# Two-layer decoder trunk: weight differences taken two per gate/up pair behind each product, and the first FFN boundary re-ordered

## The reference, cut to what matters

```
x = x + rms_norm(f(rms_norm(x, g_pre)), g_post)

def swiglu(h, w_in, w_out):
    gu = h @ w_in
    g, u = jnp.split(gu, [FFN_HIDDEN], axis=-1)
    return (jax.nn.silu(g) * u) @ w_out
```

## Time and profile before

| what | value |
|---|---|
| median of 3 runs | 1205.3 us (1205.02 to 1206.21) |
| the profiled execution's own time | 1205.84 us |
| its span, first to last instruction | 1203.9 us |
| TensorE busy | 1171.3 us (97%) |
| VectorE, ScalarE, GpSimd busy | 634.5, 445.6, 485.9 us |
| mean granted TensorE clock | 0.992 |

### The profile page before, as it was taken

One profiled execution on the slowest core, in us unless ns is written; L12 is line 12 of the kernel. 1 busy time (PEld: TensorE's weight loads), 2 busy tenths in 40 slices (PEclk: granted clock), 3 DMA queues, 4 the chain that ended last, 5 costly groups with the idle time before them and its releaser, 6 DMA issues.

```text
span 1203.9 us, 13773 instructions
## 1 busy us (share of the span) xinstructions
PE 1171.3 (97%) x5434; PEld 966.6 (80%) x5434; DVE 634.5 (53%) x783; ACT 445.6 (37%) x681; POOL 485.9 (40%) x268
## 2 busy tenths in 40 slices
PE   8999999998999999999979999999989999999998
PEld 6888887896887888888768888778968788888886
DVE  3441056274344655677365844734635356556773
ACT  5122336442222222365434333644322232225642
POOL 5546521745355544200647443023545454441004
PEclk9999999998999999999989999999999999999999
DMA  7444203256776233466644233112576752325663
GB/s 269 130 126 143 99 3 103 71 193 254 289 294 235 96 105 88 114 193 193 220 162 149 97 131 115 35 53 73 213 309 245 278 210 87 105 87 149 192 194 120
DMA packets 53085, 187.30 MB, mean 156 GB/s; under 512 B 4739, under 2 KB 4995, under 8 KB 52780
## 3 DMA queue, kind: packets, MB, share of 16 engines
q1 hardware_dynamic: 48760, 173.38, 42.4%
q10 hardware_dynamic: 4276, 13.26, 3.7%
HBM read 160.13 MB, written 26.49 MB: 155 GB/s over the span
## 4 chain that ended last, share of the span: by engine, by line
PE 78%; DMA 12%; DVE 8%; POOL 1%; ACT 1%; issue 0%; SPq 0%; DVEq 0%; POOLq 0%
PE ps L1255 23%; PE ps L1257 23%; PE ps L1256 23%; DMA stage<-fold_w 6%; DMA fold_t<-stage 5%; DVE stage L950 3%; PE ps L1520 2%; PE ps L1486 2%; DVE stage L948 1%; DVE stage L947 1%; DVE stage L949 1%; PE ps L1504 1%; PE ps L1292 1%; DMA gain_pre<-norms 1%; POOL w_lo L362 0%
## 5 line engine op out<-in xcount | busy, mean ns | idle before, releaser
L362 POOL TENSOR_TENSOR w_lo<-w_raw,w_hi 128x1024 fp32r<-128x1024 f32 (+1 forms) x179 | 443.2, 2483 | 621.1 <-ACT w_hi L478 619.2
L1255 PE MATMUL ps<-h_hi,w_hi 128*128 128x512 f32 (+1 forms) x1008 | 386.1, 383 | 11.8 <-DVE prod L972 11.8
L478 ACT ACTIVATE w_hi<-w_raw 128x1024 fp32r<-128x1024 f32 x240 | 244.7, 1031 | 388.3 <-DMA w_raw<-weights 313.5
L1256 PE MATMUL ps<-h_lo,w_hi 128*128 128x512 f32 (+1 forms) x1008 | 383.5, 380 | 0.0
L1257 PE MATMUL ps<-h_hi,w_lo 128*128 128x512 f32 (+1 forms) x1008 | 383.4, 380 | 0.0
L1255 PEld LDWEIGHTS ps<-h_hi,w_hi 128*128 128x128 f32 x1008 | 190.5, 189 | 51.2 <-issue 16.1
L1257 PEld LDWEIGHTS ps<-h_hi,w_lo 128*128 128x128 f32 x1008 | 190.5, 189 | 36.3
L1256 PEld LDWEIGHTS ps<-h_lo,w_hi 128*128 128x128 f32 x1008 | 190.6, 189 | 35.7 <-issue 0.2
L972 DVE TENSOR_TENSOR prod<-work,ps 128x512 f32<-128x512 f32 x44 | 30.1, 684 | 195.4 <-ACT work L629 195.4
L1257 PE MATMUL ps<-w_hi,prod_r 128*128 128x512 f32 x308 | 119.9, 389 | 0.0
L1255 PE MATMUL ps<-w_hi,h_hi 128*128 128x512 f32 x288 | 115.2, 400 | 0.4 <-DVE h_lo L867 0.4
(11 more groups left out here) (152 smaller groups left out, 1198.4 us busy)
## 6 DMA issues: line engine op xcount, KB each, us to landing
w_raw<-weights SPq DMA_DIRECT2D x156, 512.0 KB, 4.4
stage<-fold_w SPq DMA_DIRECT2D x10, 2048.0 KB, 8.3
fold_t<-stage SPq DMA_DIRECT2D x10, 2048.0 KB, 7.5
w_raw<-fold_t SPq DMA_DIRECT2D x40, 512.0 KB, 4.2
w_raw<-fold_w SPq DMA_DIRECT2D x30, 512.0 KB, 3.8
x<-x_in SPq DMA_DIRECT2D x4, 512.0 KB, 6.3
gain_post<-norms ACTq DMA_DIRECT2D x4, 512.0 KB, 4.2
stage<-fold_w SPq DMA_DIRECT2D x2, 1024.0 KB, 5.3
```

What stands on the lines that cost most here:

```text
L362: nc.gpsimd.tensor_tensor(w_lo[:, c % RING, 0:n], w_raw[:, c % RING, 0:n], w_hi[:, c % RING, 0:n].bitcast(F32), ALU.subtract).then_inc(lo_ ...
L478: nc.scalar.activation(w_hi[:, c % RING, 0:n], w_raw[:, c % RING, 0:n], ACT.Copy).then_inc(hi_done, 1)
L1255: mm(to, held[0], moved[0], start=start, stop=False, skip_group_check=more)
L1256: mm(to, held[0], moved[1], start=False, stop=False, skip_group_check=more)
```

## The change

Three places are touched.

- **SyncE**: the load of fold j comes behind chunk 8+4j's load instead of chunk 6+4j's, and the store of fold j behind chunk 12+4j's instead of 8+4j's, directly ahead of the load of fold j+1.
- **VectorE**: of each fold, two subtractions come behind product 2j and two behind product 2j+1; the last fold comes whole behind product 10. Each subtraction now also waits for the one before it.
- **Boundary 2**: ScalarE's post squares of tiles 0 and 1 come ahead of `high(V1)`, and the later steps of the chain follow in another order; GpSimd has the two post roots ahead of `low(V1)`; VectorE has the residual of tile 1 ahead of the normed row of tile 0; TensorE has its turn of tile 0 behind column 0 of product 6's last three chunks, and the turn of tile 1 ahead of the last chunk.

```diff
@@ SyncE
-                    j, late = divmod(c - FINS[layer] - 6, 4)
-                    if 0 <= j < FOLDS and late in (0, 2):
+                    j, late = divmod(c - FINS[layer] - 8, 4)
+                    for j, store in ((j - 1, True), (j, False)):
+                        if late or not 0 <= j < FOLDS:
+                            continue
                         part = slice(j * CHUNK, min((j + 1) * CHUNK, FH * SEQ))
                         held = stage[:, :, 0:part.stop - part.start]
-                        if late == 0:
+                        if not store:
 
                             if FOLDS * layer + j:
                                 sp.wait_ge(fold_stored, 16 * (FOLDS * layer + j))
...
@@ GpSimd, boundary
                 half_eps(b)
+                if b == 2:
+                    post_rstds(b, 0)
+                    post_rstds(b, 1)
+                    low(V1)
+                    pre_rstds(b, 0)
+                    pre_rstds(b, 1)
+                    low(V1 + 1)
+                    for t in (2, 3):
+                        post_rstds(b, t)
+                        low(V1 + t)
+                        pre_rstds(b, t)
+                    return
...
-            lows(FOUT0 + 36, V1 + 2)
+            lows(FOUT0 + 36, V1)
...
@@ ScalarE, boundary
+                if b == 2:
+                    sums(0, True, False)
+                    sums(1, True, False)
+                    high(V1)
+                    sums(0, False, True)
+                    sums(1, False, True)
+                    high(V1 + 1)
+                    turned_high(b, 0)
+                    sums(2, True, False)
+                    high(V1 + 2)
+                    turned_high(b, 1)
+                    sums(2, False, True)
+                    sums(3, True, False)
+                    high(V1 + 3)
+                    sums(3, False, True)
+                    turned_high(b, 2)
+                    turned_high(b, 3)
...
             ffn_out(0)
-            highs(V1, V1 + 2)
...
@@ VectorE, boundary
-                for t in range(2):
-                    post(b, t)
-                    pre(b, t)
+                post(b, 0)
+                if b == 2:
+                    post(b, 1)
+                pre(b, 0)
+                if b != 2:
+                    post(b, 1)
+                pre(b, 1)
                 turned_low(b, 0)
...
@@ VectorE, fold and ffn
-            def fold(layer, j):
+            def fold(layer, j, parts):
 
                 n = min(CHUNK, FH * SEQ - j * CHUNK)
                 w11, w12, w21, w22 = (stage[:, i, 0:n] for i in range(4))
-                vec.wait_ge(fold_landed, 16 * (FOLDS * layer + j + 1))
-                own(nc.vector.tensor_tensor(w11, w12, w11, ALU.subtract))
-                nc.vector.tensor_tensor(w12, w22, w12, ALU.subtract)
-                own(nc.vector.tensor_tensor(w22, w22, w11, ALU.subtract))
-                nc.vector.tensor_tensor(w21, w21, w22, ALU.subtract).then_inc(folded, 1)
+                if 0 in parts:
+                    vec.wait_ge(fold_landed, 16 * (FOLDS * layer + j + 1))
+                    own(nc.vector.tensor_tensor(w11, w12, w11, ALU.subtract))
+                    own(nc.vector.tensor_tensor(w12, w22, w12, ALU.subtract))
+                if 1 in parts:
+                    own(nc.vector.tensor_tensor(w22, w22, w11, ALU.subtract))
+                    nc.vector.tensor_tensor(w21, w21, w22, ALU.subtract).then_inc(folded, 1)
...
                 for p in range(FT):
-                    if p % 2 == 0 and p // 2 < FOLDS:
-                        fold(layer, p // 2)
...
                         nc.vector.tensor_tensor(prod_r[:, LO11, p, :], prod[:, A11, p, :],
                                                 prod_r[:, HI11, p, :].bitcast(F32), ALU.subtract).then_inc(product_ready, 1)
+                        fold(layer, p // 2, (0, 1) if p == FH - 1 else (p % 2,))
...
@@ TensorE, ffn_out
-                for t in range(2):
-                    if b < 4:
-                        turn(b, t)
-                    for i in range(3, 6):
-                        last = chunk(6, i, (4, 6), True, side(5), (t,))
-                        if t == 1:
-                            last.then_inc(chunk_used, 1)
-                    if t == 0:
-                        last.then_inc(y_done, 1)
+                for i in range(3, 6):
+                    last = chunk(6, i, (4, 6), True, side(5), (0,))
+                last.then_inc(y_done, 1)
+                if b < 4:
+                    turn(b, 0)
+                for i in range(3, 6):
+                    if b < 4 and i == 5:
+                        turn(b, 1)
+                    chunk(6, i, (4, 6), True, side(5), (1,)).then_inc(chunk_used, 1)
```

More of the change, by code:

```diff
@@ L416, in boundary @@
                 half_eps(b)
+                if b == 2:
[10 more added lines that the diff above has]
+                    return
                 post_rstds(b, 0)
-                if b in (1, 3):
+                if b < 4:
                     low(AFTER[b] + AHEAD - 1)
@@ L421, in boundary @@
                 for t in range(1, TILES):
-                    if b == 2 and t <= 2:
-                        low(AFTER[b] + t + 1)
                     post_rstds(b, t)
@@ L514, in sum_post_squares @@
                     act.wait_ge(merged, 10 * (b // 2 - 1) + 8 + t + 1)
-                if b == 4:
+                if b == 4 or (b, t) == (2, 1):
                     act.wait_ge(post_summed, q)
@@ L532, in sum_pre_squares @@
                 if b:
-                    act.wait_ge(post_summed, q - 3)
-                elif t:
+                    act.wait_ge(post_summed, q - 2 if (b, t) == (2, 0) else q - 3)
+                if (b, t) == (2, 1) or (t and not b):
                     act.wait_ge(pre_summed, q)
@@ L551, in sums @@
                         sum_pre_squares(b, t)
+                if b == 2:
[15 more added lines that the diff above has]
+                    turned_high(b, 3)
+                    act.wait_ge(x_updated, 4 * b)
+                    act.dma_start(gain_post[:], norms[b, 1].partition_broadcast(P)).then_inc(gain_post_landed, 16)
+                    return
                 sums(0, True, True)
-                if b == 2:
-                    high(AFTER[b] + 2)
                 sums(1, True, True)
-                if b == 2:
-                    high(AFTER[b] + 3)
                 if b == 0:
```

## The result

The changed kernel takes 1210.66 us (median of six runs, 1209.73 to 1211.94) against 1205.16 before: a ratio of 1.0047, 95% interval 1.0034 to 1.0060. It is slower, as forecast, but by 5.5 us and not by 28. Its profiled execution took 1211.13 us with a span of 1209.2. The two parts go opposite ways, as the prediction's sum has them: the boundary gains, the folds lose.

A forecast was written before the change was run, and what follows sets the result against it. The prediction took the one-buffer turn of load, fold, store and next load to bound TensorE: 1205.84 + 38.8 (folds, two FFNs) - 11.0 (boundary 2) = 1233.6, so 1233 us, range 1206 to 1244.

The forecast's parts named there:

- Boundary 2: Where TensorE waits for the normed row `gate_x`: the earlier chain and later turns win the full 11.0 us.
- the second half of the fold: VectorE's last two subtractions of a fold: both stand behind one of GpSimd's and take 6.74 us together.
- two meetings: Forecast's own case: both second-half subtractions wait for GpSimd; about 1224 to 1243 us, chance 0.62.
- one meeting: Rival: VectorE gets in first once, second half 4.5 us, chunk 25 at 404.9; 1211 us, chance 0.18.
- the store of 7.49 us: The fold's store back from the buffer, taken at 7.49 us as one term of each turn.
- the circle: Load, fold, store, next load through one buffer: 27.15 us a turn against 21.76 us for four chunks of TensorE.
- the first wait and its half clock: Layer 0's wait of 4.59 us for the product, and 2.2 us of clock behind it: both gone.
- the last store: End of each FFN's folds: behind chunk 32's load, product 11 waits for it; chunk 25 starts 26.2 us late.
- the loss of 9.0 us per FFN before: What each FFN's waits for the product cost TensorE in the unchanged kernel, read at silu(11): 9.0 us.
- the cover of the turns: `gate_x` of tiles 0 and 1 ready ahead of TensorE's turns, by 1.2 us or more and 1.6 us.

The follow-up runs named there:

- e6: The changed kernel with a short VectorE memset of 128 columns ahead of each split fold's second half, so that GpSimd gets in front: 1232.28 us.
- e4: The changed kernel with each fold whole, all four subtractions behind product 2j, the queue of loads and stores as changed: 1213.91 us.
- e9: The changed kernel with GpSimd's subtraction for chunk 4j+10 held until fold j is done: 1196.93 us.
- e7: The changed boundary, with the folds in eleven parts of 512 columns through both halves of the same buffer: 1175.90 us.
- e3: The changed kernel with the store of fold 5 behind chunk 30's load instead of chunk 32's: 1202.82 us.

## Why the prediction was right and where it went wrong

**The step that failed** is the second half of the fold: "GpSimd is ahead by 0.09 us, and both subtractions of the second half should stand behind one of GpSimd's: 6.74 us". It measured 4.54, with VectorE ahead by 0.08 us. The mechanism was right: whoever is first makes the other wait, and e6 with GpSimd in front gave 1232 us. The lead was read too finely from rows 7, in two ways. First, I took start plus duration of `prod_r` for the time at which VectorE can start, 310.72. In the changed kernel `prod_r` ends by its row at 304.01 + 0.99 = 305.00, and the next instruction, which waits for nothing, starts at 304.93: 0.07 us earlier. Second, the product starts 302.84 - 301.19 = 1.65 us behind the rounding of its chunk, in the earlier trace rows 1.57. GpSimd's next subtraction hangs on a rounding that follows the product, and moves with it; `prod_r`, which takes 0.42 us alone and 0.99 here, ends when GpSimd's earlier subtraction lets it (302.33 + 2.38 = 304.71), and doesn't move. Together 0.15 us, which turn +0.09 into -0.06, near the measured -0.08. This account of the lead is read from the two traces and wasn't tried apart; that the lead decides over 21 us was.

The weight of the two cases was misread, too. The prediction took two meetings "since the same pair of streams met in every turn of the first fold". The second fold of the kernel before looks different, by the timeline of VectorE and GpSimd:

```profile
292.21 1.22 DVE L949 TENSOR_TENSOR stage<-stage 128x1024 f32<-128x1024 f32 x1
293.47 3.30 DVE L950 TENSOR_TENSOR stage<-stage 128x1024 f32<-128x1024 f32 x1
...
292.23 3.45 POOL L362 TENSOR_TENSOR w_lo<-w_raw,w_hi 128x1024 fp32r<-128x1024 f32 x1 [2.86 <-ACT w_hi L478]
```

VectorE is in front by 0.02 us, and only one subtraction meets GpSimd. In the kernel before, the eight full-size folds that follow each layer's first all show these two times, 1.22 and 3.30 us; only the first fold of each layer meets GpSimd all the way. So the trace before spoke for one meeting at least as much as for two.

The Trainium skill (SBUF — State Buffer, section SBUF: two separate sides) has the shared port pair held by whoever starts first, the other fully blocked. The rows agree: 1.21 us in front and 3.30 behind, and with the order turned by 0.17 us, 3.30 for both. What a meeting costs was forecast rightly; who is first was not.

**A second term was too large**: the store of 7.49 us took 6.60. The value in the earlier trace rows came from another position in the queue: before, two chunk loads go out from 0.4 us behind the store on (297.22); in the changed kernel nothing follows on SyncE's queue until the store has landed. e4's stores directly behind a chunk load took 8.87. That the chunk loads make the difference fits these rows, but was not tried alone, and two of the changed kernel's ten stores took 7.1 and 7.2 us for no reason that the trace shows. Both terms make up the circle: 27.15 - 2.20 - 0.89 = 24.06, measured 24.1.

**Right, by rows**: from a fold's landing to the start of the second half 5.12 us forecast, 304.93 - 299.93 = 5.00 measured; the first wait and its half clock gone; the last store behind chunk 32's load, product 11 behind the store, TensorE's wait there forecast at about 6.5 us and measured at 7.5 (the 1 MB store took 6.3 us behind chunk 32's load, not 5.1); that the circle, not an engine, sets TensorE (e6, e9); the loss of 9.0 us per FFN before (e7). The rival "one meeting" had chunk 25 at 404.9 and 1211 us; they came at 407.07 and 1210.66. From silu(0) to silu(21) the loops got 9.7 and 6.9 us longer, 16.6 together, where that rival had twice 8.2, so that the sum comes out so closely is partly luck. Layer 1 loses less than layer 0 in two places. Its four turns from fold 0's landing to fold 4's take 960.04 - 863.97 = 96.1 us against 372.14 - 274.69 = 97.5. From chunk 21's start to chunk 24's end are 985.85 - 963.78 = 22.1 us against 399.53 - 375.87 = 23.7, since in layer 0 the clock fell behind chunk 21's wait of 2.44 us and in layer 1, behind 1.94 us, it did not (1.00 over 963 to 968 us).

**Boundary 2**: -11.0 forecast; alone it gave 1193.78, 12.4 us less than before beside it, of which 1.0 is fewer waits for the product (10.8 against 11.8). From silu(21) of layer 0 to silu(0) of layer 1 the changed kernel is 11.6 us shorter (344.7 against 356.2). Two details were off without effect: `gate_x` of tile 1 didn't meet `low(V1+1)` (1.28 us, not 3.45), and the cover of the turns was larger than needed.

**The chances**: 0.62 on two meetings and 0.18 on one was too sure for a lead of 0.09 us. Since the order of two engines was read from a difference smaller than the start-up differences between rows, both orders deserved about the same weight. The stated range of 1206 to 1244 held both cases; the one time that was forecast, 1233, was that of one of them.

## What to carry to other kernels

When one buffer goes round through load, work and store, add up the circle and compare it with the compute time of one turn: here 22, 24 and 26 us against 21.76 decided over 1197, 1211 and 1232 us. With the last store cured too, one buffer did as well as two halves of it (1177 and 1176). Where two engines come to a shared resource within 0.1 us, don't forecast the order from rows: price both, or settle it in the program with a wait (e9, 14 us faster than the changed kernel). A store on which a product depends should go out when its data are ready and not behind a load that waits for something later; two chunks earlier in the queue gave 8 us (e3).

## What was not expected of the hardware

An instruction of 0.17 us on VectorE, with no input in memory, was enough to let GpSimd in front; the subtraction behind it then took 3.30 us instead of 1.21. In the changed kernel an instruction of VectorE that waits for nothing started 0.07 us before the one ahead of it ends by its row (304.93 against 305.00); one that waits for the one ahead of it started 0.03 us behind that end (306.17 against 306.14). A 2 MB store took 6.6 us in eight of the ten cases of the changed kernel and 8.87 directly behind a chunk load (e4). How long TensorE waited does not by itself tell whether the granted clock falls behind the wait: in layer 0 of the changed kernel it fell behind 2.44 us (0.66 over 375 to 380 us) and behind 1.91 us (0.79 over 326 to 334), in layer 1, with three waits of 1.74 to 1.94 us, it was 1.00 over 870 to 985, and in e6 it was 1.00 over 331 to 336, behind a wait of 2.59 us. What decides is open.
